# Recurrent mixer: the last level of the inversion on 64x64 quarters, and the products with the state issued together

## The reference

```python
def step(state, inp):
    r_t, w_t, k_t, v_t, a_t, b_t = inp
    sa = jnp.einsum('bhij,bhj->bhi', state, a_t)
    state = (state * w_t[:, :, None, :] + sa[..., None] * b_t[:, :, None, :]
             + v_t[..., None] * k_t[:, :, None, :])
    return state, jnp.einsum('bhij,bhj->bhi', state, r_t)
```

## Time and profile before

| what | value |
|---|---|
| median of 3 runs | 1856.79 us (1854.01 to 1861.56) |
| profiled execution | 1854.54 us |
| its span, first to last instruction | 1852.7 us |
| mean granted TensorE clock | 0.971 |
| TensorE matmul busy | 1743.3 us, 94% |
| TensorE weight load busy | 1657.2 us, 89% |
| VectorE busy | 1004.9 us, 54% |
| ScalarE busy | 785.2 us, 42% |
| GpSimd busy | 99.2 us, 5% |

### The profile page before, as it was taken

The page is one execution under the profiler, slowest core; times in us unless marked ns, Lnnn a source line. Parts: engine busy times, 40 slices in busy tenths (PEclk is TensorE's granted clock), DMA queues, the critical chain, the costliest instruction groups (busy, mean ns, idle before and its releaser), DMA issues. The chain is left out here.

```text
span 1852.7 us, 31331 instructions
## 1 busy us (share of the span) xinstructions
PE 1743.3 (94%) x13621; PEld 1657.2 (89%) x13621; DVE 1004.9 (54%) x1286; ACT 785.2 (42%) x1118; POOL 99.2 (5%) x88
## 2 busy tenths in 40 slices
PE   7999999899999878978999998988899999999899
PEld 6989998899998868977999988888899899999899
DVE  5565453663535346365454467777646754455443
ACT  5542222633223245443343346666545533444432
POOL 2110000300000100131000000000011000000000
PEclk9999999899999989988999999999999999999999
DMA  9643232433234634535666533344455455556453
GB/s 261 182 137 83 78 90 57 128 92 92 71 90 125 153 79 162 172 112 139 185 174 171 153 114 121 118 126 133 153 182 150 147 170 154 159 149 184 141 182 114
DMA packets 252784, 254.00 MB, mean 137 GB/s; under 512 B 8865, under 2 KB 249538, under 8 KB 252264
## 3 DMA queue, kind: packets, MB, share of 16 engines
q1 hardware_dynamic: 251992, 251.80, 47.0%
q0 software_dynamic: 656, 0.21, 0.1%
HBM read 249.29 MB, written 2.69 MB: 136 GB/s over the span
## 5 line engine op out<-in xcount | busy, mean ns | idle before, releaser
L212 DVE TENSOR_TENSOR w_lo<-w_raw,w_hi 128x1024 fp32r<-128x1024 f32 (+1 forms) x452 | 549.9, 1219 | 554.7 <-ACT w_hi L207 554.6
L240 PE MATMUL ps<-xt,w_hi 128*128 128x256 f32 x2736 | 804.5, 294 | 24.0 <-DVE w_lo L212 19.8
L241 PE MATMUL ps<-xt,w_hi 128*128 128x256 f32 x2736 | 781.0, 285 | 0.0
L242 PE MATMUL ps<-xt,w_lo 128*128 128x256 f32 x2736 | 781.0, 285 | 0.0
L207 ACT ACTIVATE w_hi<-w_raw 128x1024 fp32r<-128x1024 f32 (+1 forms) x452 | 469.9, 1044 | 644.4 <-PE ps L242 519.6
L240 PEld LDWEIGHTS ps<-xt,w_hi 128*128 128x128 f32 x2736 | 532.0, 194 | 46.9 <-issue 34.5
L241 PEld LDWEIGHTS ps<-xt,w_hi 128*128 128x128 f32 x2736 | 532.0, 194 | 1.0 <-issue 0.7
L242 PEld LDWEIGHTS ps<-xt,w_lo 128*128 128x128 f32 x2736 | 531.4, 194 | 0.0
L249 PE MATMUL ps<-w_hi,xt 128*128 128x256 f32 x832 | 245.6, 295 | 0.0
L250 PE MATMUL ps<-w_lo,xt 128*128 128x256 f32 x832 | 238.3, 286 | 0.0
L251 PE MATMUL ps<-w_hi,xt 128*128 128x256 f32 x832 | 238.3, 286 | 0.0
(11 more groups left out here) (380 smaller groups left out, 1544.6 us busy)
## 6 DMA issues: line engine op xcount, KB each, us to landing
w_raw<-in_a_w_in SPq DMA_DIRECT2D x128, 512.0 KB, 3.7
w_raw<-in_w_in SPq DMA_DIRECT2D x120, 512.0 KB, 3.6
w_raw<-in_b_w_in SPq DMA_DIRECT2D x96, 512.0 KB, 3.7
w_raw<-in_w_out SPq DMA_DIRECT2D x32, 512.0 KB, 4.6
w_raw<-in_a_w_out SPq DMA_DIRECT2D x32, 512.0 KB, 3.5
w_raw<-in_b_w_out SPq DMA_DIRECT2D x32, 512.0 KB, 3.6
arena<-in_x SPq DMA_DIRECT2D x2, 1024.0 KB, 8.2
w_raw<-in_w_in SPq DMA_DIRECT2D x8, 256.0 KB, 5.9
```

The costliest lines, as they stand in the source:

```text
L212: k.nc.vector.tensor_tensor(k.wl[:, p % RING, :, 0:w], k.raw[:, p % RAW, :, 0:w], k.wh[:, p % RING, :, 0:w].bitcast(F32), ALU.subtract).th ...
L240: pe.matmul(os, h[:, cs], xt[:, kt, 0:S], start=st and ct == 0, stop=False, skip_group_check=True)
L241: pe.matmul(os, h[:, cs], xt[:, kt, S:2 * S], start=False, stop=False, skip_group_check=True)
L242: last = pe.matmul(os, l[:, cs], xt[:, kt, 0:S], start=False, stop=sp, skip_group_check=True)
```

## The change

At the last level (`lv == LV - 1`), the transposes take only the upper left 64x64 quarter of `MU` and write 64 partitions; the products with `NL` take its lower left quarter and the lower right one of `MU`, both on partitions 64 to 127, and write partitions 0 to 63; the products with `MT` take partitions 0 to 63. VectorE's mask multiplication and its addition become plain copies of 64 partitions, ScalarE's copy takes 64 partitions by 4 x 64 elements. The number of instructions stays the same there.

In the stages for c = 1, the four products with the state are issued ahead of the others, instead of one before each. As a bank is now written in one accumulation over all heads, only the first product in a bank has `start` set. (`for u in range(4 * c)` is empty for c = 0.)

```diff
@@ -625,33 +625,44 @@
             for lv in range(LV):
                 for c in range(2):
                     pe.wait_ge(dv_[c], d0[c] + 8 + 2 * lv)
-                    if lv:
+                    if lv == LV - 1:
+                        for u in range(4):
+                            m = pe.transpose(bank(c, 1)[0:64, u * P:u * P + 64], unit(buf[c][MU], u)[0:64, 0:64],
+                                             ident[0:64, 0:64])
+                        m.then_inc(mm_[c], 1)
+                    elif lv:
                         for u in range(4):
                             m = pe.transpose(bank(c, 1)[:, u * P:(u + 1) * P], unit(buf[c][MU], u), ident)
                         m.then_inc(mm_[c], 1)
                     for u in range(4):
-                        m = pe.matmul(share(bank(c, 0), u, lv), unit(buf[c][NL], u),
-                                      columns_of(buf[c][MU], u, lv), start=True, stop=True)
+                        if lv == LV - 1:
+                            m = pe.matmul(share(bank(c, 0), u, lv)[0:64, :], unit(buf[c][NL], u)[64:P, 0:64],
+                                          unit(buf[c][MU], u)[64:P, 64:P], start=True, stop=True)
+                        else:
+                            m = pe.matmul(share(bank(c, 0), u, lv), unit(buf[c][NL], u),
+                                          columns_of(buf[c][MU], u, lv), start=True, stop=True)
                     m.then_inc(mm_[c], 1)
                     yield
                 for c in range(2):
                     pe.wait_ge(dv_[c], d0[c] + 9 + 2 * lv)
                     if lv:
                         pe.wait_ge(ac_[c], a0 + lv)
+                    half = slice(0, 64 if lv == LV - 1 else P)
                     for u in range(4):
-                        m = pe.matmul(share(bank(c, 0), u, lv), unit(buf[c][MT], u),
-                                      share(buf[c][QQ], u, lv), start=True, stop=True)
+                        m = pe.matmul(share(bank(c, 0), u, lv)[half, :], unit(buf[c][MT], u)[half, half],
+                                      share(buf[c][QQ], u, lv)[half, :], start=True, stop=True)
                     m.then_inc(mm_[c], 1)
                     yield
             for c in range(2):
                 pe.wait_ge(dv_[c], d0[c] + 8 + 2 * LV)
                 if c:
                     pe.wait_ge(dv_[0], d0[0] + N_DVE[0])
+                for u in range(4 * c):
+                    pe.matmul(bank(c, 0)[:, u * 64:(u + 1) * 64], at_(hh)[ps_, u, P:S], state[ps_, u, :],
+                              start=(u == 0), stop=False, skip_group_check=True)
                 for u in range(4):
-                    o = bank(c, 0)[:, u * 64:(u + 1) * 64]
-                    if c:
-                        pe.matmul(o, at_(hh)[ps_, u, P:S], state[ps_, u, :], start=True, stop=False)
-                    m = pe.matmul(o, unit(buf[c][AK], u), tok(aa, c, u, par), start=(c == 0), stop=True)
+                    m = pe.matmul(bank(c, 0)[:, u * 64:(u + 1) * 64], unit(buf[c][AK], u), tok(aa, c, u, par),
+                                  start=(c == 0 and u == 0), stop=True, skip_group_check=True)
                 m.then_inc(mm_[c], 1)
                 yield
                 pe.wait_ge(ac_[c], a0 + LV)
@@ -667,12 +678,15 @@
                         pe.matmul(o, tok(em, 0, u, par), us[:, u * 64:(u + 1) * 64], start=True, stop=False)
                         m = pe.matmul(o, tok(ep(hh), 0, u, par), tok(aa, 0, u, par), start=False, stop=True)
                     m.then_inc(mm_[c], 1)
+                for u in range(4 * c):
+                    pe.matmul(k.ps[ps_, 2 * c + 1, u * P:(u + 1) * P], state[ps_, u, :], pr[ps_, u, P:S],
+                              start=(u == 0), stop=False, skip_group_check=True)
                 for u in range(4):
                     o = k.ps[ps_, 2 * c + 1, u * P:(u + 1) * P]
-                    if c:
-                        pe.matmul(o, state[ps_, u, :], pr[ps_, u, P:S], start=True, stop=False)
-                    pe.matmul(o, us[:, u * 64:(u + 1) * 64], unit(buf[c][RB], u), start=(c == 0), stop=False)
-                    m = pe.matmul(o, tok(aa, c, u, par), unit(buf[c][RK], u), start=False, stop=True)
+                    pe.matmul(o, us[:, u * 64:(u + 1) * 64], unit(buf[c][RB], u), start=(c == 0 and u == 0), stop=False,
+                              skip_group_check=True)
+                    m = pe.matmul(o, tok(aa, c, u, par), unit(buf[c][RK], u), start=False, stop=True,
+                                  skip_group_check=True)
                 m.then_inc(mm_[c], 1)
                 yield
 
@@ -784,7 +798,11 @@
                 for c in range(2):
                     if lv:
                         act.wait_ge(mm_[c], N_PE[c] * n + mm_at(lv) + 1)
-                        nc.scalar.activation(quad(buf[c][MT]), quad(bank(c, 1)), ACT.Copy).then_inc(ac_[c], 1)
+                        if lv == LV - 1:
+                            nc.scalar.activation(quad(buf[c][MT])[0:64, :, 0:64], quad(bank(c, 1))[0:64, :, 0:64],
+                                                 ACT.Copy).then_inc(ac_[c], 1)
+                        else:
+                            nc.scalar.activation(quad(buf[c][MT]), quad(bank(c, 1)), ACT.Copy).then_inc(ac_[c], 1)
                     yield
                 for c in range(2):
                     yield
@@ -933,15 +951,21 @@
                 mask = con[:, K_LV + (lv + 1) * P:K_LV + (lv + 2) * P]
                 for c in range(2):
                     dve.wait_ge(mm_[c], m0[c] + mm_at(lv) + (2 if lv else 1))
-                    nc.vector.tensor_tensor(packed(buf[c][QQ], lv), packed(bank(c, 0), lv),
-                                            all_columns(mask, lv, 0), ALU.mult).then_inc(dv_[c], 1)
+                    if lv == LV - 1:
+                        nc.vector.tensor_copy(packed(buf[c][QQ], lv)[0:64], packed(bank(c, 0), lv)[0:64]).then_inc(dv_[c], 1)
+                    else:
+                        nc.vector.tensor_tensor(packed(buf[c][QQ], lv), packed(bank(c, 0), lv),
+                                                all_columns(mask, lv, 0), ALU.mult).then_inc(dv_[c], 1)
                     yield
                 for c in range(2):
                     b = buf[c]
                     dve.wait_ge(mm_[c], m0[c] + mm_at(lv) + (3 if lv else 2))
                     dve.wait_ge(dv_[c], d0[c] + 8 + 2 * lv)
-                    nc.vector.tensor_tensor(all_columns(b[MU], lv), all_columns(b[MU], lv),
-                                            packed(bank(c, 0), lv), ALU.add).then_inc(dv_[c], 1)
+                    if lv == LV - 1:
+                        nc.vector.tensor_copy(all_columns(b[MU], lv)[0:64], packed(bank(c, 0), lv)[0:64]).then_inc(dv_[c], 1)
+                    else:
+                        nc.vector.tensor_tensor(all_columns(b[MU], lv), all_columns(b[MU], lv),
+                                                packed(bank(c, 0), lv), ALU.add).then_inc(dv_[c], 1)
                     yield
             yield
             yield
```

## The result

| | before | changed |
|---|---|---|
| median | 1857.39 us (4 executions) | 1844.45 us (1843.03 to 1845.42, 4 executions) |
| ratio | | 0.993, 95% interval 0.9913 to 0.9948 |
| profiled execution, span | 1854.54, 1852.7 us | 1843.03, 1841.2 us |
| mean granted clock | 0.971 | 0.973 |

The kernel is 0.7% faster: 12.9 us in the medians, 11.5 in the profiled pair. A second measurement on another occasion gave 0.9931 (0.9917 to 0.9944). The forecast was 10.0 us and 1846.8, its range 1842.5 to 1853.0.

What follows compares the result with a forecast made beforehand. TensorE's instruction stream was taken to bound the mixer; 6.8 us from grouped state and output products plus 3.2 from the quarters gave 10.0, so 1844.5 us profiled, 1846.8 beside the median, range 1842.5 to 1853.0.

Steps and rivals of the forecast that it cites:

- TensorE's stream sets the time, and no stage waits: Recurrent mixer's four groups: TensorE's queue length goes straight into the end as long as no stage begins to wait.
- A new wait for `arena`: Sign of being wrong: TensorE newly waiting for `arena` or `proj` in the changed kernel's waits.
- (1): State stage, c = 1: state products issued together save six row-count changes at 0.16 us; 0.9 us a group taken.
- (2): Output stage, c = 1: the same grouping saves six changes at 0.14 us; 0.8 us a group taken.
- a price for each change of the number of rows: State and output stages: each switch between 64-row and 128-row products costs 0.16 and 0.14 us.
- (3): Last level on quarters, c = 0 and 1, four groups: 0.40 us saved eight times, 3.2 us.
- 0.8 to 0.9 named as its sign: Last level's first block in the changed timeline should take 0.8 to 0.9 us instead of 1.24.
- the way in and out: Last level's 64-column blocks: entering costs 0.09 us more than a normal step, leaving too.
- the quarters bring nothing: Rival, last level: row-half change drains the array (0.16, eight times 1.3 us), slower 64-row instructions; 1850.0 us, chance 0.19.
- The overlap of the two halves: Last level, upper bound: transposes and products on different row halves overlap, 0.24 us a block, 1.9 in all; chance 0.03.
- Transposes stay in one pass: Last level: each 64-column transpose stays one instruction, four to a block; two-pass rival costs 2.0 us, chance 0.07.
- (4): VectorE and ScalarE work on half the partitions; TensorE does not wait for them, so gain 0.

Runs made afterwards that it cites:

- same_half: Changed kernel, but last-level products with `NL` taken from partitions 0 to 63, the transposes' half, so not computing the inverse; median 1844.72 us, ratio 0.9937.
- plain_turn: Changed kernel, but the last level's four transposes made ordinary products with the identity, two instructions each; 1844.18 us (one execution).

## Why the prediction was right, point by point

- *TensorE's stream sets the time, and no stage waits.* Right inside the groups: their windows have no gap, and each pair of groups gives its 4.6 us of blocks. That the whole span shrank by 8.8 us for 9.1 us of blocks is luck, 1.5 gained and 1.8 lost by the clock. And not everything that TensorE's queue gains "goes straight into the end": between the second and the third group TensorE waits for what VectorE and ScalarE make, and the two long waits there grew by 2.5 us. A new wait for `arena`, which the prediction named as a sign of being wrong, is there too (L570, 0.2 us), but in the preparation, not in a stage.
- *(1) and (2), a price for each change of the number of rows.* Right in mechanism and size: 0.9 and 0.8 us were forecast, 0.84 and 0.86 measured, 6.8 us in four groups both ways. Pairs of products gave the straight line that a price for each change asks for. 64-row instructions with 64 moving columns run at 0.112 us, between the 0.101 and 0.125 that I had as bounds. The products with `AK` in the same stage take 0.112 too, not 0.101; so of the 0.72 us for a pair of kinds 0.45 are instructions, and a change costs 0.14 and not 0.16.
- *(3), the quarters.* Right in kind, too large: 0.40 us for the two blocks together, where 0.295 was measured, so 2.4 us and not 3.2. The first block takes 0.94 us from its first row, outside the 0.8 to 0.9 named as its sign, the second 0.61. The instruction's price was right (0.058 against 0.061 taken from the earlier trace rows), and so was the way in and out. What I left out is the step between one-pass transposes and two-pass products inside a 64-column tile, 0.14 us a block. In the full array that step costs nothing: four transposes at 0.109 and eight products at 0.101 make up the whole of 533.83 to 535.07, and I carried that over. The rival "the quarters bring nothing" named a cost of this size at this place, but laid it to the change of rows, which same_half excludes.
- *The overlap of the two halves*, my upper bound from the earlier trace rows, does exist between ordinary products, as plain_turn shows; it does not come with one-pass transposes.
- *Transposes stay in one pass.* Right: L630 x4 in 64*64. The Trainium skill's rule that column tiling excludes the fp32 transpose mode (TensorEngine Tiling (Array Packing), Restrictions and Gotchas) is not what the trace shows if it is read as two passes; what the transposes do cost in such a tile is the step of 0.14 us.
- *(4), nothing from VectorE and ScalarE.* Right. VectorE's copies of 64 partitions take the 0.42 us that the 128-partition operations took.
- *The sum.* 9.1 us of blocks for 10.0 forecast. The medians moved by 12.9, and I had no term for the rest; by the blocks alone the time would have been 1848.3 us, and that 1844.45 lies in the range too is owed to a lower end that was drawn for the overlap and the scatter. The rest goes along with the mean granted clock. Executions of before at a mean clock of 0.973 or more took 1853.1 us on average (4 of 39), those of the changed kernel 1843.9 (7 of 10), 9.2 apart, near the blocks' sum, though from four executions of before; below 0.973 they took 1858.4 (35) and 1847.9 (3), 10.5 apart. Most executions of before are below 0.973, most of the changed kernel's are not. That the clock makes the difference is not shown by this, and why the two kernels differ in it is open: neither the mixed stages nor lateness alone accounts for it in the runs above.

## What to carry to other kernels

When TensorE never waits, price a reordering by the distances between starts in the timeline: group small products by the rows and columns of the array that they use, since each change costs some 0.14 us here, and pad a 64-row operand with zeros where that spares the change altogether. Smaller tiles alone bring little when each block has to enter and leave them (0.09 us each way here against 0.04 us won for each instruction). Judge a gain of a few us by block lengths in the trace first: here medians moved by 1 us less to 5 us more than the blocks, and single executions of one kernel lay over 9 us apart. And where a span has shrunk by about the sum of its blocks, follow one instruction after another all the same: here a gain and a loss by the clock had cancelled, and a third gain had gone into a wait for other engines.

## What the runs showed of the hardware that I had not expected

- Two fp32 passes on 64 rows and 64 columns follow one another at 0.058 us, and streams on the two halves of the rows start 0.005 us apart when all are ordinary products; after one-pass transposes they don't overlap, and the first product comes 0.146 us later.
- A VectorE copy of 64 partitions by 256 elements takes as long as the operations with two operands on 128 partitions by 256 (0.42 us).
- A stretch at half clock ahead of a wait cost nothing: in all fourteen profiles TensorE waits 2.5 us for `w_lo` behind such a stretch near 325 us and 3.8 us without one.
- Executions of one kernel differ in the mean clock that TensorE is granted: with 0.9 us of work added, five took 1842.68 to 1846.05 us at 0.973 to 0.975 and the sixth 1851.92 at 0.970.
